# Differential attention in float32: 1/rms of q as a factor on the scores, and the k and output norms' roots over 192 columns

## The reference

```python
q = rms_norm(q.reshape(bsz, n, 2 * DIFF_HEADS, DIFF_DH), qn_g)
k = rms_norm(k.reshape(bsz, n, 2 * DIFF_HEADS, DIFF_DH), kn_g)
q_l, k_l = apply_axial_rope(q_l, cos, sin), apply_axial_rope(k_l, cos, sin)
...
s = jnp.einsum('bqnd,bknd->bnqk', q, k).astype(F32) * scale
p = jax.nn.softmax(s, axis=-1)
w = p[:, :, 0] - lam * p[:, :, 1]
o = jnp.einsum('bhqk,bkhe->bqhe', w.astype(v.dtype), v)
o = rms_norm(o, subln_g) * (1.0 - lam_init)
out = (o.reshape(bsz, n, D_INNER) * jax.nn.silu(z)) @ w_out
```

## Time and profile before

| what | us |
|---|---|
| median of 3 runs (3999.76 to 4014.48) | 4011.03 |
| the profiled execution, its own time | 4011.99 |
| its span, first to last instruction | 4010.3 |
| the differential attention, first projection to last head's norm | 1683 to 2851 |
| one step of its loop of 14 | 69.8 |
| TensorE busy in such a step | 65.3 |
| VectorE busy in such a step | 45.4 |
| ScalarE busy in such a step | 28.2 |
| a load of 128 x 128 weights, mean | 0.19 |

### The profile page before, as it was taken

How to read it: one execution, slowest core, us unless ns; L and a number is a source line. 1 busy time by engine, 2 the same in 40 slices (tenths; PEclk the granted TensorE clock), 3 DMA queues, 4 the chain that set the end, 5 groups by cost and what they waited for, 6 DMA issues and landing times.

```text
span 4010.3 us, 44586 instructions
## 1 busy us (share of the span) xinstructions
PE 3700.1 (92%) x16234; PEld 2354.2 (59%) x16234; DVE 2045.9 (51%) x3693; ACT 1197.8 (30%) x2200; POOL 143.2 (4%) x227
## 2 busy tenths in 40 slices
PE   5998999998889999899999999998798999999989
PEld 2445488873446888665656565564454555555554
DVE  3744353644545545455666666666214555555541
ACT  1213210112332101133434434343102454545530
POOL 6600000000000000000000000000000000000000
PEclk8998999999999999999999999999899999999999
DMA  7521334340013342410111011100011122212211
GB/s 149 143 75 48 95 95 106 89 112 24 21 53 105 95 116 74 116 37 27 32 31 31 26 31 31 31 26 26 23 51 58 53 58 58 58 53 57 58 32 53
DMA packets 456433, 246.27 MB, mean 61 GB/s; under 512 B 44256, under 2 KB 448352, under 8 KB 456320
## 3 DMA queue, kind: packets, MB, share of 16 engines
q1 hardware_dynamic: 420384, 216.15, 19.6%
q0 software_dynamic: 14144, 28.36, 2.7%
q10 hardware_dynamic: 21792, 0.22, 0.4%
HBM read 229.83 MB, written 14.80 MB: 61 GB/s over the span
## 4 chain that ended last, share of the span: by engine, by line
PE 79%; DVE 12%; ACT 4%; issue 2%; ACTq 1%; DMA 0%; DVEq 0%; SPq 0%
PE bank L466 19%; PE bank L1188 15%; PE bank L328 10%; PE bank L1709 8%; DVE rs L1934 4%; PE bank L1695 3%; PE bank L1036 3%; PE bank L1100 3%; PE bank L863 2%; PE bank L1731 2%; PE bank L1081 2%; PE bank L1742 2%; PE bank L846 1%; PE bank L1677 1%; PE bank L1345 1%
## 5 line engine op out<-in xcount | busy, mean ns | idle before, releaser
L1188 PE MATMUL bank<-hT,ring 128*128 128x512 f32 (+1 forms) x1664 | 634.1, 531 | 11.3 <-ACT hT L1599 6.0
L1709 PE MATMUL bank<-hT,ring 128*128 128x512 f32 x1504 | 509.0, 490 | 20.0 <-DVE big L1961 16.3
L1188 PEld LDWEIGHTS bank<-hT,ring 128*128 128x128 f32 x1664 | 311.1, 191 | 289.0 <-issue 276.2
L1709 PEld LDWEIGHTS bank<-hT,ring 128*128 128x128 f32 x1504 | 280.6, 190 | 244.4 <-issue 207.1
L328 PE MATMUL bank<-big,ring 128*128 128x512 f32 (+1 forms) x1024 | 389.2, 543 | 12.3 <-DVE big L1973 8.4
L328 PEld LDWEIGHTS bank<-big,ring 128*128 128x128 f32 x1024 | 195.8, 192 | 204.2 <-issue 183.9
L1088 ACT ACTIVATE arena<-bank 128x512 f32<-128x512 f32 (+2 forms) x224 | 118.4, 528 | 462.3 <-PE bank L1081 462.0
L466 PE MATMUL bank<-big,arena 128*128 128x256 f32 x1024 | 228.8, 379 | 0.0
L466 PEld LDWEIGHTS bank<-big,arena 128*128 128x128 f32 x1024 | 194.6, 190 | 26.5
L1056 DVE CUSTOM_DVE_ANT_0 arena<-bank,big 128x512 f32<-128x512 f32 (+2 forms) x152 | 101.3, 666 | 201.4 <-PE bank L1036 201.4
L1695 PEld LDWEIGHTS bank<-ring,hT 128*128 128x128 f32 x1536 | 179.2, 193 | 30.4 <-DVE arena L1928 17.1
(11 more groups left out here) (293 smaller groups left out, 5276.0 us busy)
## 6 DMA issues: line engine op xcount, KB each, us to landing
ring<-in_mlp_w SPq DMA_DIRECT2D x128, 512.0 KB, 5.5
ring<-in_a_w_in SPq DMA_DIRECT2D x64, 512.0 KB, 4.0
ring<-in_b_w_in SPq DMA_DIRECT2D x64, 512.0 KB, 4.0
ring<-in_mod_w SPq DMA_DIRECT2D x48, 512.0 KB, 4.0
ring<-in_even_w_in SPq DMA_DIRECT2D x32, 512.0 KB, 4.0
bias_d<-tb POOLq DMA_DIRECT2D x96, 128.0 KB, 3.3
big<-bias_d POOLq DMA_DIRECT2D x16, 768.0 KB, 5.4
ring<-in_a_w_out SPq DMA_DIRECT2D x16, 512.0 KB, 3.7
```

The source lines that it names most:

```text
L1188: mm = pe.matmul(bk(b + n)[0:m, 0:z - a], ring[s][:, k, 0:m], (rhs or hcol)(k, a, z), start=k == 0, stop=k == kt - 1)
L1709: mm = pe.matmul(flatb[2][:, a:z], ring[s][:, k, :], hT[:, k, a:z], start=k == 0, stop=k == KT - 1)
```

## The change

- The factor 1/rms of q is no longer multiplied into q. q is rotated as it comes from the projection, with the gain of its norm folded into the rotation matrix (`rotq`) and into the other operand. The factor is computed with tokens on partitions: the squares are the stationary operand and two columns (one for each half-head) the moving one, six products of 2 columns each (`stats_q`), root and reciprocal over 12 columns. It enters the scores as the `scale` of the exponentials and as a factor on the negated maxima.
- The sums of the k and the output norm are computed as four products with 32 output partitions, each for a quarter (192) of the tokens, so that quarter j lies on partitions 32j to 32j+31. Root and reciprocal run over 192 columns. Four products with a selection matrix (64 rows deep, 192 columns) spread the result to 128 partitions x 768 tokens in bank 3 (`broadcast`), and VectorE reads it there.
- The order on TensorE: the rotation of q moves ahead of the projection of k; the statistics of k move one v tile forward; the statistics of the output move ahead of the z tiles 2 and 3, directly behind the rotation of k; the two broadcasts are new, one in the v projection and one behind z tile 3. On VectorE the rotation of q moves between maxima 1 and probabilities 1, and reciprocal and norm of the output move ahead of the maxima of the context block.
- A second small transfer brings the selection matrices (128 x 256), and TensorE waits for both transfers and for `rotq` once, ahead of the stage.

```diff
-        STEP = ["Tc'", "T0", "sq", "T1", "rq", "sk", "T2", "rk", "so'", "T3"]
+        STEP = ["Tc'", "T0", "rq", "sq", "T1", "sk", "bk", "T2", "rk", "so'", "bo'", "T3"]
...
                 pe.wait_ge(ds["sq"], n)
                 st.n_free(pe, x)
-                for a, z in spans(TT):
-                    mm = pe.matmul(flatb[3][:, a:z], lhs, d_sq[:, a:z], start=True, stop=True)
+                for j in range(4):
+                    mm = pe.matmul(flatb[3][32 * j:32 * j + 32, 0:G], lhs, d_sq[:, G * j:G * j + G],
+                                   start=True, stop=True, skip_group_check=True)
                 mm.then_inc(ds["st"], 1)
+            def stats_q():
+                pe.wait_ge(ds["sq"], st.sq["q"])
+                st.n_free(pe, "sq")
+                for t in range(6):
+                    mm = pe.matmul(flatb[3][:, 2 * t:2 * t + 2], d_sq[:, P * t:P * t + P], per_head,
+                                   start=True, stop=True, skip_group_check=True)
+                mm.then_inc(ds["st"], 1)
+            def broadcast(x, n):
+                pe.wait_ge(ds["rr"], n)
+                st.n_free(pe, x)
+                for i in range(2):
+                    for half_, r in enumerate((LO, HI)):
+                        mm = pe.matmul(bank[3][:, half_, G * i:G * i + G], sel[i][r, :], d_rn[r, :],
+                                       start=True, stop=True, skip_group_check=True)
+                mm.then_inc(ds["bc"], 1)
...
             if make:
+                rotate_q()
                 project(1, "k", 0, 4)
-                stats("sq", st.sq["q"], b64)
+                stats_q()
                 project(1, "k", 4, 8)
             if on:
                 turn(1, "T1", h)
                 scores(2)
             if make:
-                project(2, "v", 0, 2)
-                rotate("rq", g * 2 + 1)
-                project(2, "v", 2, 4)
-                stats("sk", st.sq["k"], b64)
-                project(2, "v", 4, 6)
+                project(2, "v", 0, 1)
+                stats("sk", st.sq["k"], b64[:, 48:80])
+                project(2, "v", 1, 5)
+                broadcast("bk", st.rr["k"])
+                project(2, "v", 5, 6)
             if on:
                 turn(2, "T2", h)
                 scores(3)
             if make:
                 project(3, "z", 0, 2)
-                rotate("rk", g * 2 + 2)
+                rotate_k()
+            if old:
+                stats("so'", st.sq["o'"], ones[:, 0:32])
+            if make:
                 project(3, "z", 2, 4)
             if old:
-                stats("so'", st.sq["o'"], ones)
+                broadcast("bo'", st.rr["o'"])
             if make:
                 project(3, "z", 4, 5)
...
             def root(n, w):
                 act.wait_ge(ds["st"], n)
-                act.activation(rs[:, :], flatb[3][:, 0:TT], ACT.Sqrt, scale=1.0 / w, bias=eps).then_inc(ds["nf"], 1)
+                act.activation(d_rn, flatb[3][:, 0:G], ACT.Sqrt, scale=1.0 / w, bias=eps).then_inc(ds["nf"], 1)
+            def root_q():
+                act.wait_ge(ds["st"], st.sq["q"])
+                act.activation(d_rq[ge], flatb[3][:, 0:12], ACT.Sqrt, scale=1.0 / 64, bias=eps).then_inc(ds["nf"], 1)
...
-                dve.tensor_scalar(dst[:, 4:4 + n], dst[:, 0:n], -1.0, None, ALU.mult).then_inc(ds["nm"], 1)
+                dve.scalar_tensor_tensor(out=by_head(dst, 4), in0=by_head(dst, 0), scalar=-1.0, in1=f,
+                                         op0=ALU.mult, op1=ALU.mult).then_inc(ds["nm"], 1)
...
+            def inverse(x, n):
+                st.n_done(dve, x)
+                dve.reciprocal(d_rn, d_rn).then_inc(ds["rr"], 1)
+            def normed_k():
+                dve.wait_ge(ds["bc"], st.rr["k"])
+                dve.scalar_tensor_tensor(out=spread(d_nrm), in0=spread(d_raw), scalar=cols[:, 6:7],
+                                         in1=bank[3][:, :, 0:2 * G], op0=ALU.mult, op1=ALU.mult).then_inc(ds["nr"], 1)
...
             if make:
-                evac(0, 0)
+                evac(0, d_q)
             if on:
                 maxima(1)
+            if make:
+                rotated_q()
+            if on:
                 probs(1)
             if make:
-                normed("q", 0, 5)
-                evac(1, 1)
+                evac(1, d_raw)
+                inverse_q()
             if on:
                 maxima(2)
                 probs(2)
             if make:
-                rotated(0, [(dq_(ge), ALL)])
-                normed("k", 1, 6)
+                inverse("sk", "k")
+                normed_k()
             if on:
                 maxima(3)
                 probs(3)
             if make:
-                rotated(1, [(dk_(ge), ALL)])
+                rotated_k()
             if old:
                 gated(h - 1, 1 - e, "o'", "pv'")
+                inverse("so'", "o'")
+                y_normed(h - 1, "o'", "so'")
             if on:
                 maxima(4)
                 probs(4)
-            if old:
-                y_normed(h - 1, "o'", "so'")
...
-            sp.dma_start(part(9984, 1024), d["consts"][:, C_AX:C_END]).then_inc(ds["ax"], 16)
+            sp.dma_start(part(9984, 1024), d["consts"][:, C_AX:C_SEL]).then_inc(ds["ax"], 16)
+            sp.dma_start(cst[:, C_CZ:C_CZ + 256], d["consts"][:, C_SEL:C_END]).then_inc(ds["ax"], 16)
```

More of the change, by code:

```diff
@@ L87, in constants @@
     c[:, C_AX + 512:C_AX + 1024] = np.tile(np.sin(ang), (2, 1))
+    for p in range(P):
+        if p % 16 == 0:
+            o = C_SEL + 128 * (p // 32 % 2) + 64 * (p // 16 % 2)
+            c[p, o:o + 64] = 1.0
     return c
@@ L1618, in program, with spread @@
         d_raw, d_nrm, d_sq = part(7680, TT), part(8448, TT), part(9216, TT)
+        d_q = rs[:, :]
+        G = TT // 4
+        tbf = tb[:, :, :].rearrange("p a b -> p (a b)")
+        d_rn = tbf[:, 0:G]
+        d_rq = [tbf[:, G + 12 * e:G + 12 * e + 12] for e in range(2)]
+        sel = [cst[:, C_CZ + P * i:C_CZ + P * i + P] for i in range(2)]
+        rotq = cst[:, C_RP:C_RP + P]
+        per_head = b64.rearrange("p (s n) -> p s n", s=2)[:, :, 0]
+        def spread(x):
+            return x.rearrange("p (a n) -> p a n", a=2)
         axc = [part(9984, 512), part(10496, 512)]
@@ L1841, in act_dif @@
             if make:
-                if old:
-                    act.wait_ge(ds["y"], h)
-                root(st.sq["q"], 64)
+                root_q()
             if on:
@@ L1940, in rotated @@
-            def rotated(n, write):
-                dve.wait_ge(ds["rot"], g * 2 + (n + 1))
-                dve.tensor_tensor(d_t2, bank[3][:, 0, :], axc[1], ALU.mult).then_inc(ds["nf"], 1)
-                for dst_, r in write:
-                    mm = dve.tensor_copy(dst_[r, S:TT], d_nrm[r, S:TT])
-                dve.tensor_tensor(d_nrm[:, 0:S], d_nrm[:, 0:S], axc[0], ALU.mult).then_inc(ds["m1"], 1)
-                dve.wait_ge(ds["m1"], g * 2 + (n + 1))
-                st.n_done(dve, "rq" if n == 0 else "rk")
-                for dst_, r in write:
-                    mm = dve.tensor_tensor(dst_[r, 0:S], d_nrm[r, 0:S], d_t2[r, :], ALU.add)
-                mm.then_inc(ds["m2"], 1)
+                dve.wait_ge(ds["m2"], g * 2 + j)
@@ new lines, in rotated_q @@
+            def rotated_q():
+                dve.wait_ge(ds["rot"], g * 2 + 1)
+                dve.tensor_tensor(d_t2, bank[3][:, 0, :], axc[1], ALU.mult).then_inc(ds["nf"], 1)
+                dve.tensor_scalar(dq_(ge)[:, S:TT], d_q[:, S:TT], cols[:, 5:6], None, ALU.mult)
+                dve.scalar_tensor_tensor(out=dq_(ge)[:, 0:S], in0=d_q[:, 0:S], scalar=cols[:, 5:6], in1=axc[0],
+                                         op0=ALU.mult, op1=ALU.mult).then_inc(ds["m1"], 1)
+                dve.wait_ge(ds["m1"], g * 2 + 1)
+                st.n_done(dve, "rq")
+                dve.tensor_tensor(dq_(ge)[:, 0:S], dq_(ge)[:, 0:S], d_t2, ALU.add).then_inc(ds["m2"], 1)
@@ new lines, in rotated_k @@
+            def rotated_k():
+                dve.wait_ge(ds["rot"], g * 2 + 2)
+                dve.tensor_tensor(d_t2, bank[3][:, 0, :], axc[1], ALU.mult).then_inc(ds["nf"], 1)
+                dve.tensor_copy(dk_(ge)[:, S:TT], d_nrm[:, S:TT])
+                dve.tensor_tensor(d_nrm[:, 0:S], d_nrm[:, 0:S], axc[0], ALU.mult).then_inc(ds["m1"], 1)
+                dve.wait_ge(ds["m1"], g * 2 + 2)
+                st.n_done(dve, "rk")
+                dve.tensor_tensor(dk_(ge)[:, 0:S], d_nrm[:, 0:S], d_t2, ALU.add).then_inc(ds["m2"], 1)
```

89 lines of the change are left out of this document (52 added, 37 removed).

## The result

The changed kernel takes 4049.2 us (median of 4 runs, 4041.6 to 4050.1), the kernel before 4006.6 in the same comparison: ratio 1.0097, 95% interval 1.0081 to 1.0113. That is 39 us slower by the ratio, and the two medians lie 42.6 us apart. The forecast was 4032 with a range of 4005 to 4056, so 21 us of slowdown, about half of what came. Profiled execution against profiled execution it is 4048.99 against 4011.99: +37.0 us. The differential attention, from its first projection to the output product, holds all of it: 1681.76 to 2887.47, 1205.7 us, against 1683.01 to 2851.62, 1168.6: +37.1.

A forecast was written before the change was run, and what follows sets the result against it. TensorE was taken as the bound (79% of the chain), wide VectorE reciprocals hiding pauses. Longer loop steps 12.5, clock falls 15.4, and head and first step -6.4 us gave +21.5: 4032 us median, range 4005 to 4056.

The forecast's parts named there:

- An idle spell of 3.2 us in place of 1.8: TensorE's pause ahead of the output norm's statistics in each loop step, until VectorE has read the rotated k from bank 3.
- Another idle spell of 0.5: TensorE's pause ahead of the output's broadcast, waiting 0.5 us for VectorE's gating and 1.35 us reciprocal.
- The gain ahead of the loop: Before the loop: 3.7 us gained ahead of and at the first head, 2.7 in the first step, together -6.4.
- the sum of a step: One loop step: 1.8 us lost behind block 3's scores less 0.9 gained before, so 0.9 longer; 12.5 over 14 steps.
- I take nothing, and 0.1 us for each exponential as the other end.: Price of q's factor as a second per-row operand in the exponentials: nothing, at most 0.1 us each.
- TensorE's work stays as it was.: TensorE's products in a loop step: 4.0 us added against 3.9 removed.
- The stretch behind the scores of block 3: Loop step from block 3's scores to the last z part: 14.4 us against 12.6, a loss of 1.8.
- The boundary that I drew: Clock falls after pauses like 2.88 us, not 2.70; so 3.2 us costs a net 1.1 each step, 15.4 in all.
- The last head: Final head: a 1.0 us gain, +4.4 ahead of block 3's transpose and -3.7 behind the last statistics; nearly nothing left.
- rival of the clock that holds: All as forecast but without the 15.4 us of clock loss: 4017 us; chance 0.22.
- rival of dearer products: q's statistics 2.3 us, tiled products 0.4 more where unhidden, clock low longer: +1.2 a step, 4050 us; chance 0.17.
- faster rival: Reciprocals hold the output norm's statistics, so pauses of 1.79 and 0.82 us go: 3968 us; over 20 us faster, chance 0.07.

The follow-up runs named there:

- run without the factor: Changed kernel with q's factor left out of the exponentials and the negated maxima, so q enters the scores unnormed: 4044.6 us, 1.0092 of the kernel before.
- swapped kernel before: Kernel before, wide norms kept, with VectorE's rotation of k moved between maxima 3 and probabilities 3: 3985.1 us, 0.9931 of the kernel before.
- version with the late broadcast: Changed kernel with k rotated early and also the output's broadcast moved behind the context block's scores: 3966.0 us, 0.9899 of the kernel before.
- run with doubled products: Changed kernel with each tiled statistics product, for k and the output, issued twice in a row: 4081.6 us, 1.0173 of the kernel before.
- filled pause: Changed kernel with three unread 512-column products ahead of the output norm's statistics in the loop steps: 4037.5 us, 1.0079 of the kernel before.
- rotation of k early: Changed kernel with k rotated directly behind block 3's scores on TensorE and before probabilities 3 on VectorE: 4016.4 us, 1.0021 of the kernel before.

## Why the prediction was right, and where it was wrong

The side was right, and so was the mechanism of the main loss. "An idle spell of 3.2 us in place of 1.8": 3.29. "Another idle spell of 0.5": 0.51. "No idle ahead of v": none. "Reciprocals of 1.35 us": 1.345. TensorE's small products: 1.26 us for the statistics of q (1.1 taken, and not the 0.3 of the estimate beside it), 0.46 for a tiled one (0.6), 0.85 for a broadcast (0.85). Each was released by the instruction that was named. The gain ahead of the loop was 5.5 us (6.4). The size was right only in part: the loss was twice the forecast one.

What failed is the sum of a step: 0.9 us at full clock was forecast, 2.23 came. By stretch, up to the end of block 3's scores -0.43 came in place of -0.9, from there to the last z part +2.31 in place of +1.8, and ahead of the context transpose +0.35 in place of nothing. The terms, each from one start to the next:

- "I take nothing, and 0.1 us for each exponential as the other end." It was the other end, 0.09. In the chain of block 3 that lengthens the pause by 0.17 (3.29 against 3.12), and the four exponentials of the context block lengthen theirs by 0.35, which became a new pause of 0.43 ahead of the context transpose. I had put that pause down as not touched by the change; the row that would have warned me is the 0.08 us by which the transpose missed it before. The run without the factor shows both. The Trainium skill has this price (ScalarE: Activation LUTs, What ACT_TABLE_LOAD costs: 93 ns for each operand given as one value per partition); the 87 to 89 ns here agree. With it in the sum, the step would have been forecast 0.2 to 0.5 us longer.
- "TensorE's work stays as it was." The products themselves did (3.9 us); their neighbours did not, and TensorE's work grew by 0.69 us. The three pieces of v now take 1.98 + 7.35 + 1.89 = 11.2 us (2052.13 to 2054.11, 2054.57 to 2061.92, 2062.77 to 2064.66) against 10.8 in the kernel before (3.67 + 3.57 + 3.57), 0.4 us more, and so this stretch gave 0.4 us and not 0.9. The step of the earlier trace rows has 32 halves of v between products of the full 128 x 128:

```profile
2052.28 3.73 PE L1695 MATMUL bank<-ring,hT 128*128 128x128 f32 x32
2055.85 1.46 PE L1742 MATMUL bank<-arena,cst 128*128 128x512 f32 x4
```

  They take 3.57 us to the next start, so 16 take 1.79. With a tiled product (32 columns or 64 rows) on one side 16 halves take 1.89, with one on both sides 1.98, and 64 halves with both 7.35 in place of 7.14. z tiles do the same: eight halves take 2.59 with none (2194.55 to 2197.14 in the swapped kernel before), 2.67 with one (2182.32 to 2184.99 in the version with the late broadcast). So each side on which a tiled product stands costs an untiled stretch about 0.1 us, and each of the four new tiled products has two such sides: 4 x 0.2 = 0.8, near the 0.69. The prediction says that no row shows a single change's price, yet the 3.67 and 3.57 of v in the kernel before do. The Trainium skill states a drain on a change of tiling (TensorEngine Tiling (Array Packing), Key Properties), with which this agrees; the run with doubled products shows that the surplus does not grow with the number of tiled products in a row.
- The stretch behind the scores of block 3 was summed with 1.3 for a z tile and 1.7 for transposes and scores. It takes 7.00 + 3.82 + 0.85 + 1.39 + 1.82 = 14.9 us, where 14.4 was forecast and the kernel before takes 12.6. Of the 0.5 too much, 0.25 lie ahead of the statistics (7.00 for 6.75), with the exponentials' 0.17 in them.

The clock went the other way: 15.4 us forecast, 9.7 measured, because it fell in 8 steps and not in all. Per fall about 1.1 us was right in seven of them (1.0 to 1.1, and 2.3 in one). The boundary that I drew, between pauses of 2.7 and 2.88 us, does not exist in that form: 3.29 us held in 6 steps of 14, and 1.68 us fell in 4 of 14. The last head cost 1.6 us where I had nearly nothing. The two errors of the loop, +18.7 and -5.7, and the 2.5 of its ends give the 15.5 us between 37.0 and 21.5. That the two errors of the loop have opposite signs is luck: with a fall in every step the same sum would have missed by 6 us more.

The rival of the clock that holds is not what happened, but its time was measured by the filled pause: 4037, not 4017, since the step's sum was off. The rival of dearer products comes nearest in time, 4050, and has part of the cause: each tiled product does cost more than was summed, 0.2 us beside it and not 0.4. Its other parts are absent (1.26 us for the statistics of q and not 2.3, a clock that stayed down longer in one step alone). Of the faster rival the prediction said that it decides if bank 3 is free within 3.5 us of the scores. The rotation of k early frees it 2.8 us after them, and the time is 4016; only with the broadcast late as well is it 3966, near the 3968. So the release was needed, but did not decide alone.

## What to carry to other kernels

Before an operation is made shorter, find which wait of the bounding engine it ends. Here three reciprocals of 5 us could be cut to 1.35 without touching the wait that cost most, 1.79 us a step, and one exchange of two blocks on VectorE in the old kernel was worth 26 us. A shared buffer whose release stands behind a softmax should be read before it; and each further hand-over (root, reciprocal, broadcast, norm) needs the engine's own work put between, or it shows up whole. A small tiled product has a second price, in the untiled products beside it, and is best put next to another one of its kind.

## What was not expected of the hardware

- A second per-row operand on an activation costs 0.09 us each (0.897 to 0.986 us for 768 columns, 0.473 to 0.560 for 256), for the wide as for the narrow.
- A tiled product (32 columns or 64 rows) costs the untiled products beside it about 0.1 us on each side: 16 halves of v take 1.79, 1.89 and 1.98 us with none, one and two such sides. Two tiled products in a row pay it once.
- The clock does not follow the length of a single pause. 1.79 us never lowered it in the loop of the kernel before; 1.68 us did in 4 steps of 14, pauses of 0.71, 1.80 and 1.17 us close together did in 6 of 14, 3.12 us in 14 of 14, and 3.29 us in 8 of 14 in the changed kernel but in 14 of 14 with the doubled products. Each count is of one execution. What the products on either side (32 columns or 64 rows wide) have to do with it was not tried.
- A fall is cheap or dear by what follows: 1.0 us where a wait of 0.51 us stood behind it, 1.6 us in the step with the early rotation, 2.3 us where it lasted longer.
- Twelve halves with 2 moving columns and their own 128 x 128 weights take 1.26 us, 0.105 us each: about as long as halves with 128 moving columns (3.57 us for 32 of v, 0.11 each).
